# Latent scores on one full-height tile per head, and inner norms applied behind the products of their first two units

## The chip, the cores and the metric

One NeuronCore of one Trainium2 chip. The metric is the device time of one execution in microseconds (us). Engines: TensorE (PE in the rows; PEld is its weight load), VectorE (DVE), ScalarE (ACT), GpSimd (POOL) and SyncE (SP), which issues the weight DMAs.

## What is computed

Two layers of a first block and two layers of a second block over 512 tokens of 1024 channels; the first block also carries 256 context tokens (updated in its layer 0 only). The parts that the change touches:

```python
# first block, each layer: modulation, latent attention (8 heads)
mod_x, mod_c = silu(c) @ w_mod[i] + b_mod[i], silu(c_ctx) @ w_mod[i] + b_mod[i]
q  = (rms_norm(q_lat, g_qa) @ w_qb).reshape(B, T, 8, 64 + 32)     # 64 nope, 32 rope
kv = (rms_norm(kv_lat, g_kva) @ w_kvb).reshape(B, T, 8, 64 + 64)  # 64 nope, 64 value
s = einsum('bqhd,bkhd->bhqk', q_n, keys_n) + einsum('bqhd,bkd->bhqk', q_r, keys_r)
p = softmax(s * (64 + 32) ** -0.5)                                # 768 keys; context queries: 256
o = einsum('bhqk,bkhd->bqhd', p, vals)
# second block, each layer
mod = silu(c) @ w_ada[l] + b_ada[l]                               # sh1 sc1 g1 sh2 sc2 g2
h = rms_norm_2(x, norm_g[l, 0]) * (1 + sc1) + sh1
x = x + g1 * (mix(h @ w_in[l]) @ w_out[l])
h = rms_norm_2(x, norm_g[l, 1]) * (1 + sc2) + sh2
x = x + g2 * conv_ffn(h, w_up[l], conv_w[l], conv_b[l], w_down[l])
```

## The kernel before

Everything is fp32. A weight *unit* (mostly 128 output channels by 1024 inputs, 512 KB) is loaded by SP into one of three RAW tiles; ScalarE rounds it to a high part (WH, L1551) and GpSimd subtracts to get a low part (WL, L2064); there are two WH/WL slots. Activations are split likewise: HH by ScalarE (L1580), HL by VectorE (L2235). A product is three matmuls per 128 input channels, HH·WH, HL·WH, HH·WL (`channels`, L621, eight k steps at full width). Channels lie on partitions, tokens along the free dimension.

Each engine's instructions are emitted by a program of its own, in a fixed order, and meet on semaphores. On ScalarE and GpSimd, `ahead(key)` emits the splits of the coming unit at that place of their order. Four PSUM tiles of 128x1024 go round in the order of `open_group`; a group opens when the reader of the tile's previous use has evacuated it. SP's DMAs go in the order of the list `units`, each behind the consumer of the RAW tile that it overwrites.

**Latent attention** (PE L983, ACT L1625, DVE L2372). For each pair of heads (j) and each block of 128 queries (qb) there is a unit: four pairs times four blocks with 768 keys, and in layer 0 eight more units of context queries with 256 keys. The two heads' nope rows are the two 64-row halves of QNP[:, j] and KNP[:, j], their rope rows are 32-row groups of QRP and KR. The scores of one head for 512 (or 256) keys are a 64-row product (L1000) and a 32-row product (L1004) accumulated onto it; the two heads alternate in both. VectorE takes the row maximum (L2381), ScalarE the exponential into PR (L1645), PE turns it (L1016), ScalarE and VectorE copy the turned halves into PT (L1636, L2389), PE multiplies with the values (L1033). PE's order in step n is: scores(n), transposes of head 0 of unit n-1, values of unit n-2, transposes of head 1 of unit n-1. In `latent_projections` (L950) each pair has its own weight unit `wqk`, with the q and the k weights of two heads.

**Modulation columns** (`modulation_columns`, L655). VectorE sums modulation rows over k into 128x1024 tiles (L2308). Each finished (chunk, vector) is summed over partitions by eight matmuls of a 128x128 block with a column of ones (L664, output one column wide; the trace shows 16 instructions), into one PSUM group for all vectors of a chunk; `modulation_biases` (L2312) adds the bias column (L2321).

**Inner norms of the second block.** The norms are called ("2", l, "n", i): i=0 ahead of `recurrence`, i=1 ahead of the feed-forward. For (0,1), (1,0) and (1,1), `sum_accumulated` (L718) sums squares over partitions with N=1 products (L688), the inverse root of each token is made in a column, spread over partitions by L734, with filler products (`keep_going`, L695) around it. Then VectorE makes GV = XT·SC·rstd (L2242), ScalarE HH2 = GV + shift (L1580), VectorE HL2 (L2235), for eight k in turn, and `two_units` (L738) runs the first two weight units interleaved, each k as soon as its HL2 is there. XT is the residual stream, written by VectorE at L2792 (out) and L2826 (down).

In the feed-forward, u is evacuated by ScalarE (L2029), VectorE adds two convolution taps (L2807, L2809), ScalarE applies silu (L2033), VectorE multiplies (L2817), ScalarE and GpSimd split the result (L1573, L2072).

## Time and profile before

| | |
|---|---|
| Median of three runs | 3334.89 us (3323.96 to 3335.82) |
| Profiled execution | 3332.77 us, span 3331.0 us, mean granted TensorE clock 0.967 |
| Busy shares | PE 95%, DVE 44%, ACT 35%, POOL 31% |
| Latent stage of layer 0 | 299.2 to 461.0 us |
| Latent stage of layer 1 | 1336.6 to 1462.6 us |
| Last output product to next full-rate unit, norms (0,1), (1,0), (1,1) | 25.9, 24.2, 24.7 us |

Times in the rows are us from the start of the span unless marked ns. A timeline row can merge like instructions: start, time they cover, count. `[0.49 <-ACT PR L1645]` is idle time of the engine just before the row, and what ended it. The granted clock is a share of 2.4 GHz; 0.5 is the lower level, 1.2 GHz, and a value between is a mixture in time.

### The profile page before, as it was taken

The page shows a single profiled execution, that of the slowest core. Times are in us where ns is not written, and L with a number is a line of the kernel's source. Part 1 is how long each engine was busy: PE and PEld are TensorE (multiplying, and loading weights), DVE is VectorE, ACT ScalarE, POOL GpSimd, SP SyncE. Part 2 cuts the span into 40 slices and gives each one's busy share as a digit, 9 for nine tenths or more (in the row PEclk, how much of TensorE's full clock was granted, in tenths as well). Part 3 has the DMA queues.
Part 4 walks back from the last instruction along what each step waited for, and adds up shares of the span by engine and source line. Part 5 has one row for each costly group of instructions (what it writes and reads, how often), then busy time and mean ns, then how long its engine had stood idle before and what let it go on. Part 6 is the DMA issues. An engine that isn't in the chain of part 4 may idle for free.

```text
span 3331.0 us, 45135 instructions
## 1 busy us (share of the span) xinstructions
PE 3170.3 (95%) x18436; PEld 2505.5 (75%) x18436; DVE 1466.9 (44%) x1805; ACT 1164.0 (35%) x1873; POOL 1045.1 (31%) x489
## 2 busy tenths in 40 slices
PE   8989999999999889899999999999999899999999
PEld 6766568888888667468887777678888777778887
DVE  4352335453231445442331476647762575544420
ACT  3253331211123335333223443634432334534431
POOL 1301013322343121014445232035554322135553
PEclk9998899999999899899999999999999999999999
DMA  6201004343222124224433222026655312023332
GB/s 205 44 2 40 1 26 120 89 116 94 64 58 64 34 64 107 64 73 118 114 95 89 78 57 75 12 81 185 183 178 153 89 45 78 2 82 95 101 93 92
DMA packets 442377, 279.77 MB, mean 84 GB/s; under 512 B 113610, under 2 KB 419516, under 8 KB 441788
## 3 DMA queue, kind: packets, MB, share of 16 engines
q1 hardware_dynamic: 442172, 276.87, 29.5%
q8 instruction: 148, 2.42, 0.3%
q14 instruction: 57, 0.47, 0.0%
HBM read 274.73 MB, written 2.10 MB: 83 GB/s over the span
## 4 chain that ended last, share of the span: by engine, by line
PE 70%; DVE 4%; ACT 3%; POOL 3%; issue 2%; DMA 1%; SPq 0%; ACTq 0%; DVEq 0%; POOLq 0%
PE ps L621 50%; PE ps L1184 4%; POOL WL L2064 2%; PE ps L1260 2%; PE ps L1282 1%; PE ps L1253 1%; PE ps L664 1%; PE ps L751 1%; ACT WH L1551 1%; PE ps L1000 1%; PE ps L1321 1%; PE ps L1004 1%; ACT PR L1645 1%; PE ps L1352 1%; DVE GV L2242 1%
## 5 line engine op out<-in xcount | busy, mean ns | idle before, releaser
L2064 POOL TENSOR_TENSOR WL<-RAW,WH 128x1024 fp32r<-128x1024 f32 (+2 forms) x366 | 876.4, 2395 | 1955.0 <-ACT WH L1551 1953.2
L621 PE MATMUL ps<-HH,WH 128*128 128x512 f32 (+1 forms) x2184 | 727.7, 371 | 13.8 <-POOL WL L2064 13.6
L621 PE MATMUL ps<-HL,WH 128*128 128x512 f32 (+1 forms) x2184 | 719.6, 367 | 0.0
L621 PE MATMUL ps<-HH,WL 128*128 128x512 f32 (+1 forms) x2184 | 718.7, 367 | 0.0
L1551 ACT ACTIVATE WH<-RAW 128x1024 fp32r<-128x1024 f32 (+2 forms) x366 | 377.4, 1031 | 417.4 <-PE ps L621 289.7
L621 PEld LDWEIGHTS ps<-HH,WH 128*128 128x128 f32 x2184 | 377.0, 189 | 94.1 <-POOL WL L2064 21.1
L621 PEld LDWEIGHTS ps<-HH,WL 128*128 128x128 f32 x2184 | 376.6, 189 | 70.0
L621 PEld LDWEIGHTS ps<-HL,WH 128*128 128x128 f32 x2184 | 376.5, 189 | 68.4 <-issue 0.7
L2308 DVE SCALAR_TENSOR_TENSOR XT<-RAW,CS,XT 128x1024 f32<-128x1024 f32 x77 | 134.5, 1747 | 27.6 <-DMA RAW<-in_w_ada 26.6
L621 PE MATMUL ps<-FH,WH 128*128 128x512 f32 x352 | 137.9, 392 | 2.2 <-POOL WL L2064 2.0
L621 PE MATMUL ps<-FH,WL 128*128 128x512 f32 x352 | 137.2, 390 | 0.0
L621 PE MATMUL ps<-FL,WH 128*128 128x512 f32 x352 | 137.2, 390 | 0.0
L2381 DVE TENSOR_REDUCE NMAX<-ps 128x1 f32<-128x768 f32 (+1 forms) x80 | 64.4, 846 | 147.8 <-PE ps L1004 147.8
L2308 DVE SCALAR_TENSOR_TENSOR MSUM<-RAW,CS,MSUM 128x1024 f32<-128x1024 f32 x63 | 109.0, 1767 | 4.2 <-DMA RAW<-in_w_mod 2.3
L2826 DVE SCALAR_TENSOR_TENSOR XT<-ps,MOD,XT 128x512 f32<-128x512 f32 x16 | 12.0, 751 | 200.5 <-PE ps L621 200.5
L1000 PE MATMUL ps<-KNP,QNP 64*128 64x256 f32 (+1 forms) x288 | 73.4, 587 | 24.0 <-ACT PR L1645 22.4
L1184 PE MATMUL ps<-HH,WH 128*128 128x512 f32 x208 | 91.4, 440 | 3.8 <-POOL WL L2064 3.3
L1636 ACT ACTIVATE PT<-ps 128x768 f32<-128x768 f32 (+1 forms) x40 | 29.0, 726 | 174.8 <-PE ps L1016 174.8
L2072 POOL TENSOR_TENSOR FL<-GV,FH 128x512 fp32r<-128x512 f32 x44 | 57.5, 1308 | 85.8 <-ACT FH L1573 85.8
L2029 ACT ACTIVATE UB<-ps,VEC 128x512 f32<-128x512 f32 x44 | 34.3, 780 | 140.1 <-PE ps L621 138.2
L1184 PE MATMUL ps<-HH,WL 128*128 128x512 f32 x208 | 82.2, 395 | 0.0
L1184 PE MATMUL ps<-HL,WH 128*128 128x512 f32 x208 | 82.2, 395 | 0.0
(378 smaller groups left out, 5237.4 us busy)
## 6 DMA issues: line engine op xcount, KB each, us to landing
RAW<-in_w_in SPq DMA_DIRECT2D x122, 512.0 KB, 3.8
RAW<-in_w_ada SPq DMA_DIRECT2D x96, 512.0 KB, 3.9
RAW<-in_w_up SPq DMA_DIRECT2D x88, 512.0 KB, 4.2
RAW<-in_w_in SPq DMA_DIRECT2D x72, 256.0 KB, 3.6
RAW<-in_w_mod SPq DMA_DIRECT2D x32, 512.0 KB, 3.7
RAW<-in_w_down SPq DMA_DIRECT2D x32, 512.0 KB, 4.1
WMOD<-in_w_mod SPq DMA_DIRECT2D x8, 1024.0 KB, 14.5
RAW<-in_w_branch SPq DMA_DIRECT2D x16, 512.0 KB, 3.5
```

The costliest lines, as they stand in the source:

```text
L621: ins = nc.tensor.matmul(ps[0:width, t0:t0 + tn], a, b[:, k0 + k, t0:t0 + tn], start=first and k == 0 and i == 0, stop=last and k == kt - ...
L664: ins = nc.tensor.matmul(ps[:, c:c + 1], total[:, j // 2, j % 2 * P:j % 2 * P + P], ones[:, 0:1], start=True, stop=True)
L751: ins = nc.tensor.matmul(groups[n][:, t0:t0 + tn], a, b[:, k, t0:t0 + tn], start=k == 0 and t == 0, stop=k == KD - 1 and t == 2)
L1000: nc.tensor.matmul(halves[h][:, c:c + m], QNP[hs, j, qs], KNP[hs, j, start:start + m], start=True, stop=False)
L1184: ins = nc.tensor.matmul(ps[:, 0:SEQ], lhs, rhs[:, k, 0:SEQ], start=k == 0 and i == 0, stop=k == KD - 1 and i == 2)
L1260: ins = nc.tensor.transpose(ps[:, b * P:(b + 1) * P], P2[n % 2][h][:, b * P:(b + 1) * P], ident)
L1551: A(WH[s % NWS][:, 0:used], RAW[n % NRAW][:, 0:used], ACT.Copy).then_inc(*up(w_high))
L2029: A(U[:, :], ps[:, 0:SEQ], ACT.Identity, bias=vec("conv_b", l, c), scale=vec("conv2", (l, 1), c)).then_inc(*up(act_out, ("2", l, "u", j, s)))
L2064: nc.gpsimd.tensor_tensor(WL[s % NWS][:, 0:used], RAW[n % NRAW][:, 0:used], WH[s % NWS][:, 0:used].bitcast(F32), ALU.subtract).then_inc(*u ...
L2072: nc.gpsimd.tensor_tensor(L, GV[n % 2][:, 0:T], H.bitcast(F32), ALU.subtract).then_inc(*up(split_low, key))
L2308: V.scalar_tensor_tensor(total, row, c, total, ALU.mult, ALU.add).then_inc(*done)
L2381: V.tensor_reduce(NMAX[:, 2 * n + h:2 * n + h + 1], ps[:, 0:keys], AX.X, ALU.max, negate=True).then_inc(*up(to_act, ("B", l, n, h)))
```

## The change

**A, norms.** For the three norms (0,1), (1,0), (1,1), `late_units` takes the place of `sum_accumulated` and `two_units`. ScalarE and VectorE write HH2/HL2 = split(XT·SC), without rstd and shift, k by k inside the preceding wout or down loop. The first two units multiply these at once; the shift goes through the same weights as a two-column product into columns 512:514 of the same PSUM tile; column sums and the spreading of rstd stand between their products. VectorE then forms (product · rstd) + shift term into UT or FS (`late_value`), and ScalarE and VectorE read it there. The normalised values overwrite HH2/HL2 afterwards, for all later units. Fillers of these norms go.

**B, latent scores.** Each head has a 128-row tile QS/KS: 64 nope rows, 32 rope rows, 32 rows of zeros in Q. Scores are one product per head and key range, the heads one after the other, each with a PSUM group opened in its turn. The zero rows are written by GpSimd behind the last window-attention unit, four of them ahead of each `wq` split. Probabilities of odd units go to a part of the weight tiles, of even units to GV. `wqk` x4 becomes `wq` x2 and `wk`; evacuations are two half-height copies on ScalarE; VectorE rotates q into QS head by head and copies the rotated key to each head's KS.

**C, modulation columns.** The eight N=1 products of a (chunk, vector) become eight 128x128 transposes into a full PSUM tile, one group for each vector, and VectorE reduces 128x1024 to eight columns ahead of the bias add.

The core of the diff (shared indentation taken off):

```diff
         pe.wait_ge(mod_summed, at(mod_summed, chunk + (KD - 1,)))
-        ps = open_group(chunk)
         for v in range(len(vectors_of(chunk))):
-            total = sum_tile(chunk, v)
+            ps, total = open_group((chunk, v)), sum_tile(chunk, v)
             for j in range(CHUNK // P):
-                c = v * CHUNK // P + j
-                ins = nc.tensor.matmul(ps[:, c:c + 1], total[:, j // 2, j % 2 * P:j % 2 * P + P],
-                                       ones[:, 0:1], start=True, stop=True)
-        ins.then_inc(*up(product_ready, chunk))
+                ins = nc.tensor.transpose(ps[:, j * P:(j + 1) * P], total[:, j // 2, j % 2 * P:j % 2 * P + P],
+                                          ident)
+            ins.then_inc(*up(product_ready, (chunk, v)))
...
+def late_units(norm, first, load, acc, sq, H, L):
+    keys = late_keys(norm)
+    units.append((keys[1], load, True))
+    led.events["unit", keys[1]] = len(units) - 1
+    n_split = sum(1 for u in units if u[2])
+    pair = [first, (WH[(n_split - 1) % NWS], WL[(n_split - 1) % NWS])]
+    total, spread = open_group(norm), open_group((norm, "rows"))
+    groups = [open_group(key) for key in keys]
+    for i in range(KD + LATE_LAG):
+        for n, k in ((0, i), (1, i - LATE_LAG)):
+            if not 0 <= k < KD:
+                continue
+            if n == 0:
+                pe.wait_ge(first_low, at(first_low, (norm, "first", k)))
+                if k == 0:
+                    pe.wait_ge(to_pe, at(to_pe, (norm, "shift")))
+            elif k == 0:
+                pe.wait_ge(w_low, n_split)
+            w = [x[:, k * P:(k + 1) * P] for x in pair[n]]
+            for t, weight in enumerate(w):
+                nc.tensor.matmul(groups[n][:, 512:514], weight, SHIFT2[:, k, :], start=k == 0 and t == 0,
+                                 stop=k == KD - 1 and t == 1)
+            for t, (a, b) in enumerate(((w[0], H), (w[0], L), (w[1], H))):
+                ins = nc.tensor.matmul(groups[n][:, 0:SEQ], a, b[:, k, 0:SEQ],
+                                       start=k == 0 and t == 0, stop=k == KD - 1 and t == 2)
+            if k == KD - 1:
+                ins.then_inc(*up(product_ready, keys[n]))
+                given_back(keys[n])
+            elif n == 1:
+                ins.then_inc(*up(product_ready, (norm, "used", k)))
+        if i == 2:
+            pe.wait_ge(to_pe, at(to_pe, norm))
+            column_sums(total, acc, ones, SEQ, True, False)
+            pe.wait_ge(act_out, at(act_out, (norm, "sq", KD - 1)))
+            column_sums(total, sq[(KD - 1) % 2], ones, SEQ, False, True).then_inc(*up(product_ready, norm))
+        if i == LATE_LAG - 1:
+            pe.wait_ge(to_pe, at(to_pe, (norm, "rows")))
+            for tb in range(NXB):
+                ins = nc.tensor.matmul(spread[:, tb * P:(tb + 1) * P], RCOL[:, tb:tb + 1].to_broadcast([P, P]),
+                                       ident, start=True, stop=True)
+            ins.then_inc(*up(product_ready, (norm, "rows")))
...
-        halves = [open_group(("B", l, n, "s", h), h) for h in range(2)]
-        qs, c = slice(qb * P, (qb + 1) * P), 0
-        for i, (start, m) in enumerate(keys):
-            for h in range(2):
-                hs = slice(64 * h, 64 * h + 64)
-                nc.tensor.matmul(halves[h][:, c:c + m], QNP[hs, j, qs], KNP[hs, j, start:start + m],
-                                 start=True, stop=False)
-            for h in range(2):
-                g = 32 * ((2 * j + h) % 4)
-                ins = nc.tensor.matmul(halves[h][:, c:c + m], QRP[g:g + 32, j // 2, qs],
-                                       KR[g:g + 32, start:start + m], start=False, stop=True,
-                                       tile_position=(g, 0))
-                if i == len(keys) - 1:
-                    ins.then_inc(*up(product_ready, ("B", l, n, "s", h)))
-            c += m
+                pe.wait_ge(pool_out, at(pool_out, (l, "empty", j // 2)))
+            if j == 0:
+                pe.wait_ge(to_pe, at(to_pe, (l, "kr", "kept")))
+        qs = slice(qb * P, (qb + 1) * P)
+        for h in range(2):
+            half, c = open_group(("B", l, n, "s", h), h), 0
+            for start, m in keys:
+                ins = nc.tensor.matmul(half[:, c:c + m], QS[:, 2 * j + h, qs], KS[2 * j + h][:, start:start + m],
+                                       start=True, stop=True)
+                c += m
+            ins.then_inc(*up(product_ready, ("B", l, n, "s", h)))
...
 def norm2(l, i):
     key = ("2", l, "n", i)
+    first = ("2", l, "up", 0, 0) if i else ("2", l) + FIRST_UNITS[0]
+    if key in LATE:
+        ahead(first)
+        late_high(key, KD - 1)
     root_columns(key, SEQ, DM)
-    ahead(("2", l, "up", 0, 0) if i else ("2", l) + FIRST_UNITS[0])
+    if key in LATE:
+        rows = ready((key, "rows"))
+        A(RSTD2[:, :], rows[:, 0:SEQ], ACT.Copy).then_inc(*freed((key, "rows")))
+    else:
+        ahead(first)
     for k in range(KD):
+        if key in LATE:
+            if k == KD // 2:
+                ahead(first, 2)
+            used = (key, "used", k) if k < KD - 1 else late_keys(key)[1]
+            act.wait_ge(product_ready, at(product_ready, used))
+            if k == KD - 2:
+                ahead(first, 3)
         high_shifted(("2", l, "h", i, k), HH2[:, k, :], SEQ,
                      lambda s: MOD2[l][:, 24 * i + k:24 * i + k + 1],
-                     (key, "rows") if k == KD - 1 else None)
+                     (key, "rows") if k == KD - 1 and key not in LATE else None)
...
         ahead(key, 2)
-        value_is_there(None, ("2", l, "up", j, 0))
+        if j:
+            value_is_there(None, ("2", l, "up", j, 0))
+        else:
+            act.wait_ge(dve_step, at(dve_step, (("2", l, "up", j, 0), "taps")))
         A(UA[:, :], UA[:, :], ACT.Silu).then_inc(*up(act_out, ("2", l, "silu", j)))
         high(("2", l, "f", j), FH[:, j, :], SEQ)
+    if l + 1 < DEPTH:
...
-    for j in range(4):
-        ahead((l, "wqk", j))
+    last = len(window_units(l)) - 1
+    pool.wait_ge(product_ready, at(product_ready, ("A", l, last, "o")))
+    for t in range(2):
+        pool.wait_ge(w_low, led.count[w_low.name])
+        for head in range(4 * t, 4 * t + 4):
+            nc.gpsimd.memset(QS[empty_rows(head), head, 0:T], 0.0).then_inc(
+                *up(pool_out, (l, "empty", t) if head % 4 == 3 else None))
+            pool.wait_ge(pool_out, led.count[pool_out.name])
+        ahead((l, "wq", t))
+    ahead((l, "wk"))
...
+            ps = ready((chunk, v))
+            V.tensor_reduce(sums, ps[:, :].rearrange("p (j t) -> p j t", t=P), AX.X, ALU.add).then_inc(
+                *freed((chunk, v)))
+            own((chunk, v))
+            step(V.tensor_tensor(dst, sums, VEC[:, col:col + per], ALU.add))
...
+def late_value(norm, key, n):
+    ps, kept = ready(key), kept_late(key)
+    step(V.tensor_copy(WSHIFT[:, 0:1], ps[:, 512:513]))
+    step(V.tensor_tensor(WSHIFT[:, 0:1], WSHIFT[:, 0:1], ps[:, 513:514], ALU.add))
+    V.tensor_tensor(kept, ps[:, 0:SEQ], RSTD2[:, :], ALU.mult).then_inc(*freed(key))
+    own(key)
+    V.tensor_scalar(kept, kept, WSHIFT[:, 0:1], None, ALU.add).then_inc(*up(to_act, (key, "late")))
+    dve.wait_ge(to_act, led.count[to_act.name])
...
+    inverse_columns(norm, SEQ)
+    if norm in LATE:
+        if i:
+            modulation_rows(feed_rows(l, 0, 0))
+            modulation_rows(feed_rows(l, 0, 1))
+        own((norm, "rows"))
     apply_norm([("2", l, "h", i, k) for k in range(KD)], XT, lambda k, s: SC[:, k:k + 1],
-               lambda k, s: MOD2[l][:, 24 * i + k:24 * i + k + 1], None, HH2, HL2, SEQ,
-               (("2", l, "n", i), "rows"))
+               lambda k, s: MOD2[l][:, 24 * i + k:24 * i + k + 1], RSTD2, HH2, HL2, SEQ,
+               None if norm in LATE else (norm, "rows"))
+    if norm in LATE:
+        for n, key in enumerate(late_keys(norm)):
+            late_value(norm, key, n)
```

## Rows read from the trace of the kernel before

**Rows 1.** The page: busy time by engine; the chain, by engine

```profile
PE 3170.3 (95%) x18436; PEld 2505.5 (75%) x18436; DVE 1466.9 (44%) x1805; ACT 1164.0 (35%) x1873; POOL 1045.1 (31%) x489
...
PE 70%; DVE 4%; ACT 3%; POOL 3%; issue 2%; DMA 1%; SPq 0%; ACTq 0%; DVEq 0%; POOLq 0%
```

**Rows 2.** Timeline, a unit of layer 1: start, us, tiles, count [idle before]

```profile
1371.88 1.13 PE L1000 MATMUL ps<-KNP,QNP 64*128 64x512 f32 x4 [0.49 <-ACT PR L1645]
...
1373.99 0.70 PE L1000 MATMUL ps<-KNP,QNP 64*128 64x256 f32 x4
...
1375.26 0.87 PE L1016 MATMUL ps<-CONST,PR 128*128 128x128 f32 x6
1376.06 1.53 PE L1033 MATMUL ps<-PT,VB 128*64 128x128 f32 x24
1377.52 0.88 PE L1016 MATMUL ps<-CONST,PR 128*128 128x128 f32 x6
1378.89 1.13 PE L1000 MATMUL ps<-KNP,QNP 64*128 64x512 f32 x4 [0.49 <-ACT PR L1645]
```

**Rows 3.** Windows, latent stages: us, busy PE PEld DVE ACT POOL, clock, DMA

```profile
299.20:461.00 161.80, 146.43 (x993) 81.86 (x993) 54.02 (x73) 54.80 (x127) 0.00 (x0) 0.85 0.00 1
1336.60:1462.60 126.00, 113.29 (x833) 64.88 (x833) 62.77 (x65) 42.79 (x83) 0.00 (x0) 0.92 0.24 68
```

**Rows 4.** Groups by line: busy us, mean ns | idle before

```profile
L2381 DVE TENSOR_REDUCE NMAX<-ps 128x1 f32<-128x768 f32 x64 | 58.3, 953 | 143.2 <-PE ps L1004 143.2
...
L1645 ACT ACTIVATE PR<-ps,NMAX 128x768 f32<-128x768 f32 x64 | 56.9, 898 | 10.2 <-DVE NMAX L2381 10.2
...
L1636 ACT ACTIVATE PT<-ps 128x768 f32<-128x768 f32 x32 | 26.0, 811 | 151.7 <-PE ps L1016 151.7
...
L2242 DVE SCALAR_TENSOR_TENSOR GV<-XT,SC,ps 128x512 f32<-128x512 f32 x32 | 23.9, 748 | 11.0 <-PE ps L734 10.0
...
L943 PE MATMUL ps<-SQM,CONST 128*128 128x512 f32 x20 | 9.9, 592 | 0.0
```

**Rows 5.** The chain of waits: start us, us, engine, tile, line, count

```profile
556.88 3.46 PE ps L664 x32
...
716.48 4.51 PE ps L664 x32
...
1156.31 2.58 PE ps L943 x6
...
1296.67 4.82 PE ps L664 x32
...
1469.32 3.66 PE ps L664 x32
...
2572.82 1.68 PE ps L664 x16
...
2972.09 12.10 PE ps L621 x52
```

**Rows 6.** Timeline, start of the latent stage of layer 1

```profile
1343.18 1.99 PE L1000 MATMUL ps<-KNP,QNP 64*128 64x512 f32 x4 [3.11 <-ACT PR L1645]
...
1364.87 1.13 PE L1000 MATMUL ps<-KNP,QNP 64*128 64x512 f32 x4
```

**Rows 7.** Windows, last output product to next full-rate unit

```profile
2214.90:2240.80 25.90, 20.88 (x82) 15.69 (x82) 17.41 (x25) 10.12 (x14) 4.73 (x2) 0.87 0.25 75
2608.70:2632.90 24.20, 19.36 (x82) 14.08 (x82) 14.60 (x23) 11.17 (x16) 4.73 (x2) 0.93 0.23 71
2947.40:2972.10 24.70, 19.26 (x83) 14.16 (x82) 15.33 (x23) 10.28 (x15) 4.73 (x2) 0.93 0.15 43
```

**Rows 8.** Timeline of ACT, DVE, POOL behind the first two units

```profile
2972.92 1.28 ACT L2033 ACT_TABLE_LOAD   x1
...
2974.94 1.00 DVE L2817 TENSOR_TENSOR GV<-UA,UB 128x512 f32<-128x512 f32 x1 [1.35 <-ACT UA L2033]
...
2979.68 2.40 POOL L2064 TENSOR_TENSOR WL<-RAW,WH 128x1024 fp32r<-128x1024 f32 x1 [1.71 <-ACT WH L1551]
```

More of the change, by code:

```diff
@@ L330, in program @@
         CBIAS = place("CBIAS", [P, HEADS_2 * 896], B0 + 46)
+        UT = [place(f"UT{i}", [P, SEQ], R0 + 116 + 2 * i) for i in range(2)]
         free_columns = [XT[:, 2 * i:2 * i + 2, SEQ:NT] for i in range(4)]
@@ L947, in qr_load @@
             def qr_load(l, t):
-                return [("w_qb", l * 384, 3, (4 * t + i) * 96 + 64, 32, P, 32 * i) for i in range(4)]
+                order = sorted(range(4 * t, 4 * t + 4), key=rope_group)
+                return [("w_qb", l * 384, 3, head * 96 + 64, 32, P, 32 * i) for i, head in enumerate(order)]
             def latent_projections(l, T, first):
@@ L986, in latent_attention @@
                 N = len(us)
+                probs_slot[l] = sum(1 for u in units if u[2]) % NWS
                 def scores(n):
@@ L1775, in first_layer @@
                 for j in range(4):
-                    ahead((l, "wqk", j))
+                    if j % 2 == 0:
+                        ahead((l, "wq", j // 2))
                     key = (l, "q", j)
                     ps = ready(key)
-                    A(QNP[:, j, 0:T], ps[:, 0:T], ACT.Copy, scale=SCALE_B).then_inc(*freed(key))
+                    for head in (2 * j, 2 * j + 1):
+                        rows = nope_rows(head)
+                        ins = A(QS[rows, head, 0:T], ps[rows, 0:T], ACT.Copy, scale=SCALE_B)
+                    ins.then_inc(*freed(key))
+                ahead((l, "wk"))
+                for j in range(4):
                     key = (l, "k", j)
                     ps = ready(key)
-                    A(KNP[:, j, :], ps[:, 0:NT], ACT.Copy).then_inc(*freed(key))
+                    if j == 3:
+                        act.wait_ge(to_pe, at(to_pe, (l, "kr", "kept")))
+                    for head in (2 * j, 2 * j + 1):
+                        rows = nope_rows(head)
+                        ins = A(KS[head][rows, :], ps[rows, 0:NT], ACT.Copy)
+                    ins.then_inc(*freed(key))
                 ahead((l, "wv"))
+                act.wait_ge(to_pe, at(to_pe, (l, "qr", 1)))
                 for tb in range(NTB):
@@ L2314, in modulation_biases @@
                     name, l, c = chunk
-                    ps = ready(chunk)
                     per = CHUNK // P
+                    sums = SMALL[:, 64 - per:64]
                     for v in range(len(vectors_of(chunk))):
@@ L2350, in rotate, with latent_keys, rotate_q @@
                 V.tensor_tensor(x, x, temp[:, :], ALU.add).then_inc(*up(to_pe, done))
+                dve.wait_ge(to_pe, led.count[to_pe.name])
+            def latent_keys(l, head):
+                rows = slice(64, P) if head % 2 == 0 else slice(0, 64)
+                return V.tensor_copy(KS[head][rows, :], KR[rows, :])
+            def rotate_q(l, t, T):
+                key, x = (l, "qr_rot", t), QRP[:, t, 0:SEQ]
+                ps = ready(key)
+                step(V.tensor_tensor(T1[:, :], ps[:, 0:SEQ], sin_b, ALU.mult))
+                V.tensor_tensor(x, x, cos_b, ALU.mult).then_inc(*freed(key))
+                own(key)
+                for head in range(4 * t, 4 * t + 4):
+                    rows = rope_rows(head)
+                    ins = V.tensor_tensor(QS[rows, head, 0:SEQ], QRP[rows, t, 0:SEQ], T1[rows, :], ALU.add)
+                    if T > SEQ:
+                        ins = V.tensor_copy(QS[rows, head, SEQ:T], QRP[rows, t, SEQ:T])
+                ins.then_inc(*up(to_pe, (l, "qr", t)))
                 dve.wait_ge(to_pe, led.count[to_pe.name])
@@ L2504, in first_layer @@
                 window_attention(l)
+                latent_keys(l, HEADS_B - 2)
                 for t in range(2):
                     own((l, "qr", t))
-                    rotate((l, "qr_rot", t), QRP[:, t, 0:SEQ], cos_b, sin_b, T1, (l, "qr", t))
+                    rotate_q(l, t, T)
+                dve.wait_ge(product_ready, at(product_ready, (l, "q", 3)))
+                for head in range(HEADS_B - 2):
+                    ins = latent_keys(l, head)
+                ins.then_inc(*up(to_pe, (l, "kr", "kept")))
                 latent_attention(l)
@@ L2569, in _, with late_scale @@
                     break
+            def late_scale(norm):
+                _, l, _, i = norm
+                gain = VEC[:, COLUMN["norm2", l] + KD * i:COLUMN["norm2", l] + KD * (i + 1)]
+                step(V.scalar_tensor_tensor(SC[:, 0:KD], MOD2[l][:, 24 * i + KD:24 * i + 2 * KD], 1.0, gain,
+                                            ALU.add, ALU.mult), (norm, "scale"))
+                dve.wait_ge(act_out, at(act_out, (norm, "shift")))
+                V.tensor_tensor(SHIFT2[:, :, 1], MOD2[l][:, 24 * i:24 * i + KD], SHIFT2[:, :, 0].bitcast(F32),
+                                ALU.subtract).then_inc(*up(to_pe, (norm, "shift")))
@@ L2731, in recurrence @@
                 for n in (0, 2, 1, 3):
-                    own(("2", l, ("bff", "bfb")[n // 2], n % 2))
+                    key = ("2", l, ("bff", "bfb")[n // 2], n % 2)
+                    if late_unit(key):
+                        dve.wait_ge(act_out, at(act_out, (key, "late")))
+                    else:
+                        own(key)
                     f = FS[:, n, :]
```

152 lines of the change are left out of this document (104 added, 48 removed).

## The prediction

> **What bounds the kernel now.** First the page: TensorE is busy 95% of the span, no other engine above 44%, and the chain that ended last lies on PE for 70% [rows 1]. So time comes off where PE's own instructions get shorter, where its waits go, and where it runs at its lower clock. Only three places carry the change, and I read each by itself.
>
> The latent stages, by a window over each: 161.8 us in layer 0 with PE busy 146.4, and 126.0 us in layer 1 with PE busy 113.3; granted clock 0.85 and 0.92 [rows 3]. Full is 2.4 GHz and the other level 1.2 GHz, so 2 x 0.15 x 161.8 = 48.5 us and 2 x 0.08 x 126.0 = 20.2 us ran at 1.2 GHz. The timeline of one steady unit [rows 2] has a period of 1378.89 - 1371.88 = 7.01 us: scores 3.38 (2.11 for 512 keys, 1.27 for 256), transposes 0.80, values 1.46, transposes 0.88, and 0.49 in which PE waits for the exponential. Both heads' scores end together, so both reductions and exponentials (0.95 and 0.90 each [rows 4]) start late. At the start of the stage this costs a wait of 3.11 us [rows 6], and behind it PE is at the lower clock.
>
> The norms: 25.9, 24.2 and 24.7 us from the last output product to the next full-rate unit, PE busy 19 to 21 of them [rows 7]. The modulation columns: the chain of waits holds 14 entries of L664, six with 32 instructions and eight with 16, that is 20 (chunk, vector) sums of 16 instructions each [rows 5].
>
> **B, scores.** The trace of before has no 128-row score product, but it has a full-height fp32 one with 512 columns: six instructions take 2.58 us, 0.43 each [rows 5]. A product is two instructions, so 0.86 for 512 keys; with half the columns I take half, 0.43. A unit's scores are then 2 x (0.86 + 0.43) = 2.58 instead of 3.38. Its PE sum is 2.58 + 0.80 + 1.46 + 0.81 = 5.66 (rounded). Is there a wait left? Head 0's reduction and exponential (0.95 + 0.90) now start half a score group, 1.29 us, earlier and lie beside head 1's scores and the work behind them. ScalarE's load of a unit is 2 x 0.90 + 0.81 and about 0.4 for outputs, 3.0 us; VectorE's is 2 x 0.95 + 0.96, and in layer 1 some 1.3 of modulation rows, 4.1. Both are below 5.66, so I take none.
>
> Layer 1. Before: 1336.62 to 1364.87 for three units, 12 periods of 7.01, tail 13.55; together 125.9 [rows 2, 3, 6]. After: until the fourth unit three score groups 7.74, four half transposes 3.24, one value group 1.46, and 2.23 of waits for the first exponentials (1.05 + 0.95 + 0.23, built from the reduction and the exponential) = 14.7; then 12 x 5.66 = 67.9; tail 13.55 - 0.8 = 12.8. Sum 95.4, gain 30.5.
>
> Layer 0. Sixteen units of 768 keys and eight of 256. Scores 16 x 2.58 + 8 x 0.86 = 48.2, transposes 16 x 1.61 + 8 x 0.54 = 30.1, values 16 x 1.46 + 8 x 0.49 = 27.3; 105.6. The waits of before were 161.8 - 146.4 = 15.4; I keep 2.2 at the start and 8 around the short units, whose 1.9 us of PE work doesn't cover a reduction and an exponential. That makes 116, gain 45.7.
>
> Both sums, 76, are at 2.4 GHz. The lower clock of before stands behind waits of 1.7 to 3.1 us, which go or shrink; I leave 8 to 10 us of it, cost 4 to 5. **B: -72.** Ends: all 69 us at 1.2 GHz stay, each costing half: -42; none stays: -77.
>
> Projections: PE has the same products. Four memsets of 32 rows stand in GpSimd's queue ahead of each wq split. No row has such a memset; between nothing and 8 x 1.0 us (the width of a VectorE pass over these columns, 0.95), I take 0.75 each, mostly beside the query projections. Cost 0.8 in layer 0 and 0.3 in layer 1: **+1**. The end with all eight open would be +8 a layer, without cover for the first split only +3.
>
> A rule speaks against B. The Trainium skill, "TensorEngine Tiling (Array Packing)", When to Use Tiling, sends contractions of 64 rows to two row tiles and of 32 to four. By it the paired form is the cheap one, and B would cost. The pair of heads in this kernel takes 2.11 for 512 keys against 2 x 0.86 at full height, so the trace doesn't bear the rule out here.
>
> **C, columns.** At full clock 16 instructions take 1.68 to 1.73 (2572.82, 556.88), behind a lowered clock more: 4.51, 4.82, 3.66 for 32 [rows 5]. A transpose of 128x128 is 0.80 / 6 = 0.134 [rows 2], eight are 1.07. Seven sums inside the feed-forwards and one in a merge save 1.68 - 1.02 = 0.66 each: 5.3. The two at 1296.67: 4.82 to 2.1, -2.7; the two at 1469.32: 3.66 to 2.1, -1.5. In the four merges of layer 0 (3.46, 3.47, 4.51, 4.62) the vectors of a chunk now need a PSUM tile each, and the second waits for an evacuation by ScalarE and VectorE, about 2.1 us behind the gate product: 3.2 each, -0.3, -0.3, -1.3, -1.4. Sum **-12.7**. VectorE's reduction (0.95) hides beside 5 us products. That 32 instructions take 4.8 in one place and 3.46 in another says that PE falls to 1.2 GHz inside such a run; if it no longer does, the products behind it gain too. I put that at up to 2 us for each of the six long entries, 12, and take **-2**. End on the other side: the second tile in the merges waits longer than 2.1 us and eats C's 3.3 there.
>
> **A, norms.** `late_units` on PE: 48 products at 12.10 / 52 = 0.23 [rows 5] = 11; 32 two-column products at 0.11 = 3.6; column sums 16 x 0.11 = 1.8; spread about 1.6. That is 18. It starts 0.85 us after the last output product, when XT 7 is evacuated, and the next unit's weights come some 0.8 later: next full-rate unit after 19.7 instead of 24.7, so -5 at (1,1), -4.6 at (1,0), -6 at (0,1). The fillers that go were in PE's waiting time.
>
> What is late next: VectorE's queue is now low 7, eight pairs of 0.75 + 0.75 [rows 4], each high and low overwriting what `late_units` has read, and only then `late_value` twice, 1.6 each. It ends 23 us after XT 7. In the feed-forward u0, the taps, the table load 1.28, silu, the product 1.00 and the high part of f0 follow on ScalarE; the split of unit up(2,0) is queued behind that high part and behind u of up(1,0). It starts at about 30.8; 1.05 by ScalarE and 2.40 by GpSimd [rows 8] give 34.3. Before, up(2,0) started 34.6 after XT 7 (12.10 us behind 2972.09, less the four products of its own [rows 5]). PE has run up(1,0) and up(1,1) early and waits about 3.9 us: the gain of 5 at (1,1) is given back to 0.3, and at (0,1) likewise. In the recurrence (1,0) nothing queues behind `late_value` that PE needs at once; it keeps 4.6. **A: -5.** Ends: all three fronts kept, -16; the chain 3 us later in both feed-forwards, +1 to +3.
>
> **Sum**: -72 + 1.1 - 12.7 - 2 - 5 = -90.6; 3332.8 - 90.6 = **3242 us**. The profiled execution is 2.1 below the median, inside the 12 us that the three runs span, so I don't shift it.
>
> **The rivals.**
> 1. The norms keep their gain: PE's early units cover the chain. For it: 11 us of products lie between. Against: ScalarE's fixed order. Ten us more, 3232.
> 2. The 1.2 GHz stretches of the latent stages stay as long as they were (69 us). For it: 0.85 and 0.92 [rows 3]; the short units still wait. B is -42: 3332.8 - 42 + 1.1 - 12.7 - 5 = 3274; with half of them 3257.
> 3. A 128-row score product costs its mean duration, 592 ns [rows 4], not its step of 430. Then a long unit costs 8 x 0.16 = 1.3 more, 6.96: no gain in steady state, only at the starts. 32 x 1.3 + 8 x 0.6 = 46 less: 3288. Against: the step is what the six in a row show.
> 4. The other side: TensorE runs both latent stages at 1.2 GHz. The 196 us of PE work there (105.6 + 16 x 5.66) would take twice as long, with 8 of waits 400 instead of 287.7: +112, less 19 of the rest: 3425. It decides when more than about 103 us of the 196 run so; before, 69 of 260 busy us did. A transpose share of 1.61 in 5.66, up from 1.61 in 7.01, speaks for it; the missing waits speak against. The Trainium skill, "TensorE: Matmul & The Clock Gate", Part 4, says that transposes do not count as busy in the same way; by that the higher share would lean towards this rival. The steady units of before ran at full clock with transposes in them, which does not bear it out so far.
>
> **Chances.** Forecast 0.58, rival 1 0.15, rival 2 0.16, rival 3 0.06, rival 4 0.02, 0.03 for none of them. Range 3218 to 3282: its low end is rival 1 with the clock of the stages and of C wholly back (3232 - 5 - 10), its high end holds rival 2 and a waiting GpSimd; rivals 3 and 4 lie above. A difference of under 0.5% (17 us) can't be told from none here. Rivals 1 to 3 and the forecast are all faster: 0.95; what fits none of them is split between within (0.02) and slower, which with rival 4 has 0.03.
>
> **What would show it.** Period of a long unit in layer 1 near 5.66 with no wait for the exponential; stages of 116 and 95 us; clock above 0.95 in both. L664 entries of 1.1 us per sum. Next full-rate unit 19.7 us after the last output product, and behind up(1,1) a wait on the weights of up(2,0) of about 4 us. I am wrong if the scores of a unit take over 3 us, if the clock in the stages is 0.9 or less, or if there is no such wait.

## The result, and the profile after

The changed kernel needs 3246.2 us (median of four, 3239.0 to 3248.7), the kernel before 3332.7 in the same comparison (3324.0 to 3335.8); ratio 0.974 (0.9725 to 0.9761). The forecast was 3242 with a range of 3218 to 3282. The total fits. Of its three large terms, B (the latent scores) fits too; C (the modulation columns) and A (the norms) do not, and they are wrong in opposite directions, as the experiments show.

The page after, busy time and chain, in the form of [rows 1]:

```profile
PE 3082.0 (95%) x18057; PEld 2473.3 (76%) x18057; DVE 1563.8 (48%) x1910; ACT 1191.8 (37%) x1917; POOL 1056.1 (33%) x503
...
PE 82%; DVE 6%; POOL 4%; ACT 4%; issue 3%; DMA 1%; SPq 0%; DVEq 0%; ACTq 0%; POOLq 0%
```

The 82% can't be set against the 70% before: the shares of the chain before add up to 83% of the span only, those after to 100%, and the kernel with B alone reads 68%. What can be compared is one stretch that the chain covers in both, the latent stage of layer 1: the exponential holds 20.7% of it before and 1.1% after. One steady unit of layer 1, answering to [rows 2]:

```profile
1302.51 2.75 PE L1087 MATMUL ps<-KS,QS 128*128 128x512 f32 x8
1305.09 0.82 PE L1097 MATMUL ps<-CONST,PRS 128*128 128x128 f32 x6
1305.84 1.53 PE L1114 MATMUL ps<-PT,VB 128*64 128x128 f32 x24
1307.30 0.87 PE L1097 MATMUL ps<-CONST,PRS 128*128 128x128 f32 x6
1308.01 2.75 PE L1087 MATMUL ps<-KS,QS 128*128 128x512 f32 x8
```

The period is 1308.01 - 1302.51 = 5.50 us, without idle time (7.01 before). Scores take 2.58 as worked out; the transpose groups take 0.75 and 0.71, where the forecast of 5.66 had 0.80 and 0.81. Windows over both stages, first score to first full-rate product, as [rows 3]:

```profile
298.80:414.70 115.90, 109.28 (x833) 76.27 (x831) 55.01 (x73) 55.18 (x128) 0.00 (x0) 1.00 0.01 2
1271.50:1364.70 93.20, 88.97 (x704) 64.82 (x704) 62.95 (x65) 42.91 (x83) 0.00 (x0) 1.00 0.32 91
```

115.9 and 93.2 us, for 161.8 and 126.0 before and 116 and 95.4 in the forecast; the granted clock is 1.00 in both. The norms, windows from the last output product to the next full-rate unit, as [rows 7]:

```profile
2117.60:2137.20 19.60, 17.59 (x104) 15.20 (x104) 15.64 (x17) 7.51 (x11) 5.15 (x3) 1.00 0.37 109
2514.20:2535.40 21.20, 19.21 (x104) 16.64 (x104) 13.72 (x15) 7.52 (x11) 5.10 (x2) 0.92 0.26 81
2855.00:2874.70 19.70, 17.66 (x106) 15.25 (x105) 13.78 (x15) 7.51 (x11) 5.17 (x3) 1.00 0.18 54
```

19.6, 21.2 and 19.7 us for 25.9, 24.2 and 24.7: two of the three fronts (the stretch up to the next full-rate unit) moved to the 19.7 of the forecast; (1,0) is 1.5 longer, at a clock of 0.92. What follows them did not go as forecast. PE behind norm (1,1), and what GpSimd and VectorE do there:

```profile
2871.89 2.71 POOL L2200 TENSOR_TENSOR WL<-RAW,WH 128x1024 fp32r<-128x1024 f32 x1 [12.00 <-ACT WH L1632]
...
2872.41 2.75 DVE L2386 SCALAR_TENSOR_TENSOR GV<-XT,SC,RSTD 128x512 f32<-128x512 f32 x1
...
2875.19 0.75 DVE L2379 SCALAR_TENSOR_TENSOR HL<-GV,MOD,HH 128x512 fp32r<-128x512 f32 x1
...
2877.55 2.75 DVE L2386 SCALAR_TENSOR_TENSOR GV<-XT,SC,RSTD 128x512 f32<-128x512 f32 x1
...
2881.14 0.50 PE L660 MATMUL ps<-HH,WH 128*128 128x512 f32 x1 [2.10 <-DVE HL L2379]
...
2890.14 1.04 ACT L1632 ACTIVATE WH<-RAW 128x1024 fp32r<-128x1024 f32 x1
...
2893.68 0.80 PE L660 MATMUL ps<-HH,WH 128*128 128x512 f32 x1 [5.27 <-POOL WL L2200]
```

PE waits 2.10 us for the last HL2, and 5.27 for the weights of up(2,0); at (0,1) these are 2.11 and 8.04. And two of VectorE's eight normalising passes take 2.75 us instead of 0.75, each beside a weight split on GpSimd.

Modulation columns in the chain, answering to 716.48, 1296.67 and 2572.82 of [rows 5]:

```profile
661.38 1.09 PE ps L701 x8
...
1236.37 1.90 PE ps L701 x16
...
2478.26 0.87 PE ps L701 x8
```

In the merges of layer 0, two sums of a chunk no longer stand together: the second waits 1.12 us for its PSUM tile, until VectorE has evacuated a gate product. Both, with the wait, take 3.00 (659.23 to 662.23). The row of the second in the timeline:

```profile
661.38 1.09 PE L701 MATMUL ps<-CONST,MSUM 128*128 128x128 f32 x8 [1.12 <-DVE TME L2618]
```

### The profile page after: what moved, and what is told of

Read it like the earlier page. It is cut to its first block, busy times and chain, and to the rows that moved or that the text cites. A ratio compares the mean times of both kernels' runs of the same rounds, so it can differ in the third digit from the quotient of the medians.

```text
span 3243.1 us, 44526 instructions
## 1 busy us (share of the span) xinstructions
PE 3082.0 (95%) x18057; PEld 2473.3 (76%) x18057; DVE 1563.8 (48%) x1910; ACT 1191.8 (37%) x1917; POOL 1056.1 (33%) x503
## 4 chain that ended last, share of the span: by engine, by line
PE 82%; DVE 6%; POOL 4%; ACT 4%; issue 3%; DMA 1%; SPq 0%; DVEq 0%; ACTq 0%; POOLq 0%
PE ps L660 55%; PE ps L1265 4%; POOL WL L2200 3%; PE ps L1087 3%; PE ps L1097 2%; PE ps L1341 2%; PE ps L1114 1%; PE ps L1363 1%; PE ps L1334 1%; PE ps L1155 1%; PE ps L1145 1%; ACT WH L1632 1%; PE ps L1172 1%; PE ps L1405 1%; PE ps L818 1%
## 5 line engine op out<-in xcount | busy, mean ns | idle before, releaser
L1087 PE MATMUL ps<-KS,QS 128*128 128x512 f32 (+1 forms) x252 | 86.7, 480 | 3.6 <-ACT GV L1726 2.7
L660 PEld LDWEIGHTS ps<-FH,WH 128*128 128x128 f32 x352 | 66.0, 188 | 22.8 <-POOL WL L2200 8.2
L2158 ACT ACTIVATE UB<-ps,VEC 128x512 f32<-128x512 f32 x42 | 32.8, 780 | 130.7 <-PE ps L660 130.7
```

The source lines that it names most:

```text
L660: ins = nc.tensor.matmul(ps[0:width, t0:t0 + tn], a, b[:, k0 + k, t0:t0 + tn], start=first and k == 0 and i == 0, stop=last and k == kt - ...
L1087: ins = nc.tensor.matmul(half[:, c:c + m], QS[:, 2 * j + h, qs], KS[2 * j + h][:, start:start + m], start=True, stop=True)
L2158: A(U[:, :], ps[:, 0:SEQ], ACT.Identity, bias=vec("conv_b", l, c), scale=vec("conv2", (l, 1), c)).then_inc(*up(act_out, ("2", l, "u", j, s)))
```

## Where the time came from

By the windows the latent stages gave 45.9 and 32.8 us. The total gain is 86.6, so all the rest together gave only 8, where C and A had been put down for 20. The runs below take that apart. In them "theory 1" is the explanation that each run was made to test; its rivals are numbered behind it.

**1. Each part alone or left out** (edits: the parts of the diff as a whole).

> Keeps the latent scores (B) and the transposed columns (C); the three inner norms are as before, with sums, inverse root and normalisation ahead of the first two units. Theory 1 (A is a loss here): in the changed kernel the stretch from the last output product to the start of unit up(2,0) is 39.5 us against 35.6 before at norm (1,1) and 42.2 against 37.7 at (0,1), and the recurrence behind (1,0) and the second half of the down products of layer 0 lose about 2 and 2 us. Then taking A out gains 12 to 15 us: 3231 to 3234 against 3246. Rival (the step as forecast): A is worth -5, so this kernel needs 3251.

> Keeps A and B; modulation columns are the eight products with a column of ones as before. Theory 1 (the clock): the ones products make PE fall to 1.2 GHz, as the granted clock of 0.76 to 0.83 in six windows before against 1.00 in the same windows after says; each of the six long entries costs 2.7 to 7 us with what follows, the eight short ones 0.9. Then this kernel is 26 to 29 us slower than the changed one, 3272 to 3275, and its clock in those windows is below 0.85. Rival (the term as forecast, instruction time alone): 15 us, 3261.

> The kernel before with B alone. Theory 1: the stages are worth 46.5 and 33 us, period of a unit 5.50, and the rest moves by under 1: 3253 against 3332.7. Rival (forecast): -71, 3262. With the run without A it also gives C by difference: 20 us if the stages and the clock add up independently.

> The kernel before with C alone: latent stages and norms untouched. Theory 1: the six long entries and eight short ones give 26 to 29 us, 3304 to 3307, and the granted clock right behind the long entries is 1.00. Rival 1 (instruction time alone): -15, 3318. Rival 2: the clock gain depends on B, whose stages no longer leave PE at 1.2 GHz; then C alone gives under 15.

| kernel | median, us (lowest to highest) | ratio to before |
|---|---|---|
| A, B, C (the change) | 3246.2 (3239.0 to 3248.7) | 0.974 (0.9725 to 0.9761) |
| B, C | 3228.0 (3225.1 to 3230.6) | 0.969 (0.9662 to 0.971) |
| A, B | 3276.0 (3267.0 to 3281.9) | 0.983 (0.9791 to 0.986) |
| B | 3256.2 (3255.5 to 3260.4) | 0.977 (0.9749 to 0.9797) |
| C | 3303.0 (3294.7 to 3316.2) | 0.991 (0.9885 to 0.9941) |

In the comparisons of the last four the kernel before needs 3331.2; the change itself was measured against 3332.7. So B is worth -75.0 alone. With B alone the stages take the same 115.9 and 93.2 us as in the change; the 4 us between these 78.7 and the 75 lie outside the stages and were not followed up. C is worth -28.1 alone, -28.2 on top of B, and leaving it out of the change costs 29.8. B and C add up: B alone and C alone give 3331.2 - 75.0 - 28.1 = 3228.1, and both together need 3228.0.

A costs +18.2 on top of B and C. Marks in the PE timelines of the two profiled runs (the same instruction in both) say where, +18.4 in all: +5.2 in the feed-forward behind norm (0,1), +3.4 in the one behind (1,1), +3.1 behind (1,0) up to the end of the pair attention, and +6.7 in the product loops ahead of the three norms (+1.3, +4.1 and +1.3), in which the new kernel writes HH2 and HL2 k by k. In the down loop of layer 0 PE's waits for weight splits add up to 4.7 us where they were 2.0.

Theory 1 stands in all four against its rival, not in all its numbers. A's loss came out above its 12 to 15, C's worth within 1 us of its 26 to 29 in either run. B alone was expected at 3253 against the rival's 3262 and came out at 3256.2, nearer to the first.

**2. Why C gives twice what its instructions do.** Windows of 14 us from the start of a long entry, before, then after:

```profile
716.50:730.50 14.00, 14.00 (x74) 12.75 (x75) 10.47 (x10) 1.87 (x2) 2.79 (x1) 0.76 0.56 156
1296.70:1310.70 14.00, 13.27 (x60) 11.26 (x61) 0.88 (x4) 3.58 (x7) 4.11 (x3) 0.76 0.18 39
```

```profile
661.40:675.40 14.00, 14.00 (x83) 12.26 (x84) 12.18 (x11) 1.06 (x1) 2.39 (x1) 1.00 0.44 122
1236.40:1250.40 14.00, 12.72 (x62) 10.12 (x63) 7.05 (x12) 6.37 (x12) 8.81 (x11) 1.00 0.45 99
```

0.76 means 2 x 0.24 x 14 = 6.7 us at 1.2 GHz, which costs half of it, 3.4. From the start of the other four long entries the windows of before read 0.83, 0.83 (10 us), 0.76 (14 us) and 0.79 (8 us); together the lower clock costs 15 us there, 3.8 of it within the entries themselves, which are that much longer than 3.46. The run that keeps 16 instructions a sum, but 128 columns wide:

```diff
-  ins = nc.tensor.transpose(ps[:, j * P:(j + 1) * P], total[...], ident)
+  ins = nc.tensor.matmul(ps[:, j * P:(j + 1) * P], total[...], ident, start=True, stop=True)
```

> The changed kernel, but the eight transposes of a modulation sum are ordinary fp32 products with the identity, 128 columns wide: 16 instructions again, as with the ones, but none of them one column wide. Theory 1 (products one column wide let the clock fall): the clock stays at 1.00 behind the long entries, and only the instructions count: 8 x 2 x 0.11 = 1.7 instead of 0.9 to 1.1 per sum, 20 sums, +12 to +16 us, 3258 to 3262. Rival 1 (the clock falls with the number of instructions and weight loads, not their width): the windows behind the long entries read 0.85 or less and the time is 3272 as without C. Rival 2: a full product with 128 columns costs 0.134 an instruction, +22.

It needs 3262.7 (3260.2 to 3264.6). The window of 14 us from the start of the first pair of adjacent sums, in this kernel and in the one with A and B but not C, whose sums are still one column wide:

```profile
1242.40:1256.40 14.00, 12.72 (x71) 10.46 (x70) 5.30 (x9) 4.98 (x9) 7.21 (x8) 1.00 0.37 81
```

```profile
1251.50:1265.50 14.00, 12.75 (x57) 11.01 (x58) 1.44 (x5) 3.79 (x7) 4.29 (x5) 0.76 0.18 40
```

Clock 1.00 against 0.76, with the same number of instructions. The chain of waits has 3.77 us for the 32 instructions where transposes need 1.90, so a sum costs 0.94 more. In the four merges the second sum then waits only 0.21 instead of 1.12, and the pair costs 0.96 more: 12 x 0.94 + 4 x 0.96 = 15 us, measured 16.5. So the clock came back by the width of the products, and the rest of C by their number. This run also gives each sum a PSUM group of its own, which the kernel without C does not; section 5 changes the width and keeps the groups.

Of C's 28.1, the entries themselves hold 15.3: eight short ones go from 1.68 to 0.87 (6.5), the four pairs in the merges from 3.49, 3.49, 4.53 and 4.64 to 3.00 with the wait (4.1), the two other pairs from 4.82 and 3.66 to 1.90 (4.7). The other 12.8 stand behind the entries; the windows show 15 - 3.8 = 11 of it as clock. Theory 1 holds.

**3. VectorE stands still beside GpSimd.** The inverse root read from PSUM again:

```diff
-  A(RSTD2[:, :], rows[:, 0:SEQ], ACT.Copy).then_inc(*freed((key, "rows")))
+  A(RSTD2[:, :], rows[:, 0:SEQ], ACT.Copy).then_inc(*up(act_out, (key, "rstd")))
...
-                    own((norm, "rows"))
+                    dve.wait_ge(act_out, at(act_out, (norm, "rstd")))
...
-  apply_norm(..., RSTD2, HH2, HL2, SEQ, None if norm in LATE else (norm, "rows"))
+  apply_norm(..., None, HH2, HL2, SEQ, (norm, "rows"))
```

> The changed kernel, but VectorE's normalising pass (GV = XT x scale x inverse root) reads the spread inverse root from PSUM, as before the change, instead of its copy in SBUF. Theory 1 (a VectorE pass with two operands in SBUF stands still while GpSimd splits weights): in the changed kernel two of the eight passes of each norm take 2.75 us instead of 0.75, both beside a weight split on GpSimd of 2.7. With the operand in PSUM they take 0.75 again; the passes with HH and GV (both in SBUF) then meet GpSimd in their place, so of 4.0 us per norm I expect 2 to 3 back: the wait for HL2 of k=7 (2.1 us, three times) nearly goes, 3238 to 3243 against 3246. Rival 1: all 4 us come back in each of the three norms, 3234. Rival 2 (the 2.75 is something else, bank or code): the passes stay at 2.75 and the time at 3246.

```profile
2872.00 2.71 POOL L2200 TENSOR_TENSOR WL<-RAW,WH 128x1024 fp32r<-128x1024 f32 x1 [12.01 <-ACT WH L1632]
...
2872.51 0.75 DVE L2386 SCALAR_TENSOR_TENSOR GV<-XT,SC,ps 128x512 f32<-128x512 f32 x1
...
2873.30 1.96 DVE L2379 SCALAR_TENSOR_TENSOR HL<-GV,MOD,HH 128x512 fp32r<-128x512 f32 x1
...
2876.08 2.00 DVE L2379 SCALAR_TENSOR_TENSOR HL<-GV,MOD,HH 128x512 fp32r<-128x512 f32 x1
...
2879.70 0.50 PE L660 MATMUL ps<-HH,WH 128*128 128x512 f32 x1 [0.54 <-DVE HL L2379]
...
2892.24 0.80 PE L660 MATMUL ps<-HH,WH 128*128 128x512 f32 x1 [5.31 <-POOL WL L2200]
```

The pass with an operand in PSUM is 0.75 beside the same weight split; the next one, HL from GV and HH, both in SBUF, takes 1.96 and 2.00 in its place. The wait for HL2 falls from 2.1 to 0.54, and up(2,0) starts 1.5 us sooner behind the last output product in both layers. The time is 3243.4 (3238.6 to 3248.0): 2.8 less, inside the scatter of this run. So the mechanism and its price of 1.5 us a norm are shown by the rows, not by the total; theory 1, at the small end of the gain that it gave. The Trainium skill, "GPSIMD Engine Reference", Specifications, says that GpSimd's SBUF interface is shared with VectorE's instructions that have two SBUF inputs; these rows agree, with 2 us a pass, and the forecast had passed it over.

**4. The wait for up(2,0).** First the weight split moved ahead of f0:

```diff
+  if i and key in LATE and not feed_rows(l, 1, 0):     # ScalarE, behind the norm loop, layer 1
+      ahead(first, 4)
...
   A(UA[:, :], UA[:, :], ACT.Silu).then_inc(...)
+  if j == 0:                                           # layer 0
+      ahead(key, 3)
...
+  if i:                                                # VectorE, ahead of late_value
+      modulation_rows(feed_rows(l, 1, 0))
...
-                        if j + 1 < KF:
+                        if j + 1 < KF and (j or s):
```

> The changed kernel, but ScalarE splits the weights of unit up(2,0) ahead of the high part of f0: in layer 1 right behind the normalising loop, in layer 0 behind silu; and in layer 0 one modulation row is summed ahead of the late values, so that its RAW tile comes free and the load of up(2,0) starts some 5 us sooner. Theory 1 (the queue order on ScalarE holds up PE): the waits for the weights of up(2,0), 5.3 and 8.0 us, fall to under 1 and 3; about 3 us of it come back as a wait at up(2,1), whose split is still behind f0. Gain 4 to 10: 3236 to 3242. Rival (the feed-forward is bound by f0 itself, and PE only waits later): no change, 3246.

3244.6 (3237.7 to 3247.5), and up(2,0) starts where it did to within 0.6 us, counted from the last output product. In layer 1:

```profile
2884.39 1.06 ACT L1632 ACTIVATE WH<-RAW 128x1024 fp32r<-128x1024 f32 x1 [3.00 <-PE ps L660]
...
2890.84 1.26 POOL L2212 TENSOR_TENSOR FL<-GV,FH 128x512 fp32r<-128x512 f32 x1 [10.81 <-ACT FH L1654]
...
2892.06 4.69 POOL L2204 TENSOR_TENSOR WL<-RAW,WH 128x1024 fp32r<-128x1024 f32 x2
...
2894.47 0.50 PE L660 MATMUL ps<-HH,WH 128*128 128x512 f32 x1 [4.36 <-POOL WL L2204]
```

ScalarE rounds the weights at 2884.39, six us sooner, but GpSimd has the low part of f0 (L2212) ahead of the low part of the weights (L2204) in its own order and waits for f0 all the same. The edit moved one half of the split, so the run decides neither for theory 1 nor for the rival. The move on both engines was not tried. With the edit of section 3 added:

> Both edits: operand in PSUM and the split ahead. Theory 1: they act at different places and add: 3229 to 3238. If the cost of A is wholly these two, it reaches the kernel without A, 3228, or goes below it by the fronts' 4 to 5 us each. Rival: the chain low, normalise, late value, taps, f0 stays the longest path, and it ends at 3240 or above.

3239.5 (3234.5 to 3246.2), 3.9 less than with the operand in PSUM alone. The rows show 0.4 us of it in each feed-forward (in layer 1 up(2,0) starts 35.56 instead of 35.96 behind the first product that reads XT 7); the rest can't be told from scatter. Next, the wait left as it is, but filled:

```diff
+  if (j, s) == (2, 0):
+      ps = open_group(("2", l, "up", j, s))
+      for _ in range(20 if l else 32):
+          nc.tensor.matmul(ps[:, 512:1024], HH2[:, 0, 0:P], HH2[:, 0, 0:SEQ], start=True, stop=True)
```

> The changed kernel, with products of 512 columns whose result nobody reads in the wait ahead of up(2,0): 20 in layer 1 (4.5 us of the 5.3), 32 in layer 0 (7.3 of the 8.0). Theory 1: the wait stays, but PE no longer falls to 1.2 GHz behind it (0.72 in the six us behind it in the changed kernel), and the first product behind the fillers starts when it did: 1.5 to 3 us less in each feed-forward, 3240 to 3243 against 3246. Rival 1: the clock falls for another reason (the weight split of GpSimd runs beside it), the granted clock behind the wait stays at 0.7 and the time at 3246. Rival 2: the fillers themselves hold PE up, 3248 or more.

The 6 us from the start of up(2,0), in the changed kernel and in this one:

```profile
2893.70:2899.70 6.00, 6.00 (x20) 4.81 (x21) 0.52 (x1) 0.63 (x1) 4.00 (x2) 0.74 0.59 174
```

```profile
2893.60:2899.60 6.00, 6.00 (x26) 4.99 (x27) 0.51 (x1) 0.86 (x2) 4.00 (x2) 1.00 0.60 174
```

Clock 0.74 without and 1.00 with the fillers, and in layer 0 0.67 and 1.00. So the wait also costs the clock behind it, 2 x 0.26 x 6 / 2 = 1.6 us in layer 1 and 2.0 in layer 0. The time is 3242.8 (3237.8 to 3243.4), 3.4 less; the ranges of the two kernels overlap, but the rows of the two layers give much the same, 3.6. The operand in PSUM and the fillers at once:

> A, B and C with two of A's costs taken away at once: the inverse root read from PSUM (1.5 us a norm) and the wait ahead of up(2,0) filled (1.5 to 3 us in each feed-forward). Theory 1 (they act at different places and add, and the wait itself stays): 3236 to 3241. Then A still costs 8 to 13 us against the kernel without it, 3228. Rival (A's price is its low clock and the shared port, no more): 3231 or less.

3238.3 (3234.2 to 3241.4). They add, as far as the scatter lets one say, and A is still 10 us behind the kernel without it. What is left are the waits for up(2,0) themselves and the 6.7 us in the loops ahead of the norms, less what the fronts gain; no run takes these apart.

**5. C's lesson at another place: a version that beats both.** B and C without A; in `sum_accumulated` of the inner norms

```diff
-  matmul(ps[:, tb:tb + 1], x[:, tb * P:(tb + 1) * P], ones[:, 0:1], ...)
+  matmul(ps[:, tb * P:(tb + 1) * P], x[:, tb * P:(tb + 1) * P], ones[:, 0:P], ...)
-  A(RCOL[:, 0:T // P], ps[:, 0:T // P], ACT.Sqrt, ...)
+  A(RCOL[:, 0:T // P], ps[:, 0:T].rearrange("p (a b) -> p a b", b=P)[:, :, 0], ACT.Sqrt, ...)
```

> A version meant to beat both: B and C without A, and the column sums of the three inner norms (L688 before) 128 columns wide instead of one, the root reading every 128th column. It carries what C showed to another place: in the kernel without A the granted clock is 0.66 to 0.94 in the 10 us in which these sums stand. Theory 1 (products one column wide let the clock fall): the clock there reads 1.00, sums, fillers and spread take 1 to 2.5 us less a norm, 3221 to 3226 against 3228. Rival (the clock falls in PE's wait of 1.73 us ahead of the sums, whatever their width): clock and time unchanged, 3228.

3220.8 (3219.9 to 3224.6), ratio 0.967 (0.9657 to 0.9685): 7.2 less than without the wide sums. Norm (1,1) in the kernel without A, and then with the wide sums, each with the window of 10 us from the last output product:

```profile
2845.82 1.35 PE L725 MATMUL ps<-CONST,ACC 128*128 128x1 f32 x8 [1.73 <-DVE ACC L2343]
2847.04 1.85 PE L725 MATMUL ps<-CONST,SQ 128*128 128x1 f32 x8
...
2850.17 1.91 PE L771 MATMUL ps<-CONST,SMALL 128*128 128x128 f32 x8
...
2869.96 0.50 PE L660 MATMUL ps<-HH,WH 128*128 128x512 f32 x1 [0.95 <-POOL WL L2190]
```

```profile
2844.10:2854.10 10.00, 8.22 (x33) 7.18 (x33) 3.65 (x7) 2.98 (x5) 2.35 (x1) 0.66 0.21 59
```

```profile
2838.08 1.13 PE L732 MATMUL ps<-CONST,ACC 128*128 128x128 f32 x8 [1.73 <-DVE ACC L2354]
2839.05 1.06 PE L732 MATMUL ps<-CONST,SQ 128*128 128x128 f32 x8
...
2840.74 1.16 PE L779 MATMUL ps<-CONST,SMALL 128*128 128x128 f32 x8
...
2859.86 0.50 PE L660 MATMUL ps<-HH,WH 128*128 128x512 f32 x1 [0.95 <-POOL WL L2201]
```

```profile
2836.40:2846.40 10.00, 6.56 (x38) 5.06 (x39) 6.03 (x10) 4.01 (x6) 2.40 (x1) 1.00 0.32 91
```

From the last output product, 1.73 us ahead of the first row, to the next unit it is 25.9 and 23.5 us; at (0,1) the same 2.3 are saved, at (1,0), where the clock had fallen less (0.83 in the like window), 0.7: 5.3 of the 7.2. The clock over these 10 us is 1.00 and was 0.66, and the spread of the root, the same instructions in both, takes 1.16 instead of 1.91. The wait of 1.73 ahead of the sums, the rival's cause, is there in both.

> The best version so far (B and C without A, the column sums of the inner norms 128 columns wide), with the same width also in the post norm of layer 1 of the first block and in the first norm of the second block, whose sums stand in stretches with a granted clock of 0.84 to 0.87. Theory 1 (the column width decides): up to 1 us in each of the two, 3218 to 3221 against 3220.8, so hardly to be told from none; the first norm's 24 sums take 2.9 us instead of 3.5 in the trace. Rival (the clock falls there in the waits for the squares, 1.9 us, and not at the sums: the post norm's sums run at full speed, 0.95 and 1.05 us for eight, as they are): no change of the time, and the clock in these stretches stays where it is.

3220.3 (3215.2 to 3224.4): no difference that can be told in the total. The traces tell more. In the post norm the clock was 1.00 and stays there, and nothing is gained. In the first norm of the second block it goes from 0.66 to 1.00; the spread of the root and the window of 10 us from the first sums, before and after:

```profile
1779.53 1.91 PE L779 MATMUL ps<-CONST,SMALL 128*128 128x128 f32 x8
```

```profile
1774.50:1784.50 10.00, 10.00 (x47) 8.91 (x46) 3.56 (x7) 2.39 (x5) 0.00 (x0) 0.66 0.88 270
```

```profile
1783.38 1.16 PE L789 MATMUL ps<-CONST,SMALL 128*128 128x128 f32 x8
```

```profile
1779.40:1789.40 10.00, 8.76 (x52) 6.72 (x50) 5.28 (x10) 3.21 (x7) 0.00 (x0) 1.00 0.90 270
```

From the first of these sums to the next full-rate unit it is 1774.51 to 1799.34, 24.8 us, and then 1779.44 to 1802.41, 23.0: 1.9 saved, more than the 1 that was expected and still less than the scatter of the total. The rival, that the clock there falls in the waits for the squares, does not hold for this norm: the wait of 1.9 us is in both.

## Why the forecast was right, and where it was not

- **B, -72 for the stages and +1 for projections.** Right: -75 in all. The full-height price, no wait in the steady unit, start-up and the clock came as worked out. The stages gave 78.7 for the 72: 12 units of 5.50 instead of 5.66 are 2 us of it, and the 4 us kept for the lower clock weren't needed (1.00 in both stages). Rivals 2, 3 and 4 (a clock that stays low, a mean duration, 1.2 GHz throughout) fall for this kernel.
- **The rule of row tiles.** The Trainium skill, "TensorEngine Tiling (Array Packing)", When to Use Tiling, sends short contractions to row tiles, and the prediction took it as a rule against B. The rows show that packing did work: the 64-row products of both heads take 1.06 us together for 512 keys, less than twice the 0.86 of one full-height product. But the 32-row products cost another 1.05 (row below, to be read with [rows 2]), and one product per head that holds both parts costs 2 x 0.86 = 1.72 instead of 2.11. It is the joining of the two contractions that wins here; no run tried the packing rule with one contraction alone. The Trainium skill, "TensorEngine Tiling (Array Packing)", Key Properties, says that changing the tiling mode drains the engine. The transpose groups, 0.05 to 0.1 us shorter now that no row-tiled scores stand beside them, fit that, but no run isolates it.

```profile
1372.94 1.13 PE L1004 MATMUL ps<-KR,QRP 32*128 32x512 f32 x4
```

- **C, -12.7 and "take -2" for the clock.** The term for the entries is near (15.3; the short sums take 0.87 and not the 1.02 that was used). The pairs in the merges, with the wait for the second tile, take 3.0 where 3.2 was worked out. The clock term was mis-sized: 12.8, the upper end of 12 that the prediction gave and then set aside. The rows to size it from were at hand: a window behind a long entry shows 0.76.
- **A, -5.** Wrong in sign: +18. The fronts came nearly as worked out, and so did the mechanism that gives them back. Its sizes failed. The norm loop was counted at 0.75 a pass, but its operand moved from PSUM to SBUF, and two passes stand 2 us each beside GpSimd. So the chain behind XT 7 is longer than worked out: up(2,0) was put at 34.3 us behind it, against 34.6 before, and starts 37.9 behind it in layer 1 and 40.6 in layer 0. The wait for it was "about 3.9": it is 5.3 in layer 1 and 8.0 in layer 0, where two modulation rows of 1.28 stand between the taps. A second wait, 2.1 for HL2 behind each of the three norms, was not in the sum at all. The wait was priced at its length, without the clock behind it. At (1,0), where a gain of 4.6 stood, the front gave 3.0 and what follows took 6.1.
- **The loops ahead of the norms stood at nothing**, without a reason given, and cost 6.7 us: ScalarE and VectorE write HH2 and HL2 there between other work. In the down loop the trace shows PE waiting 1.77 once for a weight split that stands behind a late high part on ScalarE; no run isolates this. Rival 1, that the norms keep their gain, falls with the last two points.
- **Slips that move nothing:** the end of B with no lower clock is -76 by its own terms, not -77, and eight transposes are worked out as 1.07 and then entered as 1.02.
- **Luck.** The total came within 4 us because C (13 better than forecast) and B (4 better) paid for A (23 worse). That these nearly cancel was not forecast. A total that fits does not confirm its terms.

## What to carry to other kernels

In this kernel products one column wide cost more than their own time: price such products by the granted clock of the stretch behind them, and make them 128 wide where the result allows. Where the scatter of the total is wider than the gain, compare the same stretch in both traces; that found 1.9 us which the total could not show. When a step is moved, list each queue that its halves stand in; moving the ScalarE half of a weight split did nothing while GpSimd's half stayed. And before moving an operand from PSUM to SBUF, look at what GpSimd does beside the instruction that reads it.
